# Hybrid decoder trunk on one core: router under the output projection, expert outputs added tile by tile, final norm on VectorE

## The reference

```
h = h + gla_mixer(rms_norm(h, a_norm), ...)             # layer 1: stick_breaking_mixer(...)
t = rms_norm(h, m_norm[layer])
g_logits = t @ w_group + b_group                        # 4 groups, top 1
e_logits = t @ w_expert + b_expert                      # 16 experts, top 2 inside the group
for e in range(16):
    hdn = silu(t @ w_gate[e]) * (t @ w_up[e])           # 1024 -> 512
    y = y + combine[:, e:e+1] * (hdn @ w_down[e])       # 512 -> 1024
h = h + y
...
return rms_norm(h, final_norm)
```

## Time and profile before

| | |
|---|---|
| Median of 3 runs | 1294.38 us (1287.04, 1294.38, 1294.63) |
| Profiled execution, its own time | 1287.17 us |
| Its span from first to last instruction | 1285.6 us |
| PE busy | 1149.8 us (89%) |
| DVE busy | 830.1 us (65%) |
| ACT busy | 692.4 us (54%) |
| POOL busy | 150.3 us (12%) |
| Chain that ended last | PE 75%, DVE 9%, issue 7%, POOL 4% |

### The profile page before, as it was taken

One profiled execution on the slowest core, in us unless ns is written; L12 is line 12 of the kernel. 1 busy time (PEld: TensorE's weight loads), 2 busy tenths in 40 slices (PEclk: granted clock), 3 DMA queues, 4 the chain that ended last, 5 costly groups with the idle time before them and its releaser, 6 DMA issues.

```text
span 1285.6 us, 14592 instructions
## 1 busy us (share of the span) xinstructions
PE 1149.8 (89%) x5517; PEld 864.8 (67%) x5517; DVE 830.1 (65%) x843; ACT 692.4 (54%) x730; POOL 150.3 (12%) x166
## 2 busy tenths in 40 slices
PE   6999997955999999996899979989739999999992
PEld 4788875844777777774688867768627777777760
DVE  3554235276888888886523356652568888888856
ACT  3532332343877777775232226651427777777752
POOL 1200030012001010002000013430030110100012
PEclk9999988976999999998899999999859999999996
DMA  8542003118999999997112310003079999999934
GB/s 286 148 157 98 1 1 131 66 75 270 376 390 391 392 402 394 393 376 285 69 66 98 98 33 1 2 19 129 1 237 360 401 391 390 391 394 411 378 132 178
DMA packets 88948, 283.10 MB, mean 220 GB/s; under 512 B 11688, under 2 KB 11856, under 8 KB 88896
## 3 DMA queue, kind: packets, MB, share of 16 engines
q1 hardware_dynamic: 72016, 239.32, 49.5%
q0 software_dynamic: 10912, 38.67, 8.9%
q10 hardware_dynamic: 5968, 4.40, 1.0%
HBM read 259.96 MB, written 22.41 MB: 220 GB/s over the span
## 4 chain that ended last, share of the span: by engine, by line
PE 75%; DVE 9%; issue 7%; POOL 4%; ACT 2%; DMA 2%; POOLq 0%; DVEq 0%; ACTq 0%
PE ps L1293 22%; PE ps L1295 22%; PE ps L1294 22%; PE ps L1486 2%; PE ps L1311 1%; POOL xn_r L1879 1%; DMA pad<-output_table,pos 1%; DVE xn L868 1%; PE ps L1447 1%; DVE raw L1232 1%; PE ps L1514 1%; PE ps L1327 1%; DVE xT_lo L824 1%; DVE xn_r L1236 1%; POOL xn_r L1874 1%
## 5 line engine op out<-in xcount | busy, mean ns | idle before, releaser
L824 DVE TENSOR_TENSOR w_lo<-raw,w_hi 128x2048 fp32r<-128x2048 f32 x72 | 164.7, 2288 | 85.1 <-ACT w_hi L487 84.9
L487 ACT CAST w_hi<-raw 128x2048 fp32r<-128x2048 f32 x72 | 137.7, 1912 | 116.5 <-PE ps L1295 116.3
L1293 PE MATMUL ps<-w_hi,s_hi 128*96 128x512 f32 x384 | 154.9, 403 | 6.6 <-DVE s_lo L1001 6.6
L1293 PE MATMUL ps<-xT_hi,s_hi 128*96 128x512 f32 (+1 forms) x392 | 156.7, 400 | 3.5 <-DVE s_lo L1013 3.5
L824 DVE TENSOR_TENSOR xT_lo<-raw,xT_hi 128x2048 fp32r<-128x2048 f32 x64 | 146.1, 2288 | 19.4 <-ACT xT_hi L487 19.4
L1295 PE MATMUL ps<-xT_hi,s_lo 128*96 128x512 f32 (+1 forms) x392 | 155.4, 396 | 0.0
L1294 PE MATMUL ps<-xT_lo,s_hi 128*96 128x512 f32 (+1 forms) x392 | 154.4, 394 | 0.0
L1295 PE MATMUL ps<-w_hi,s_lo 128*96 128x512 f32 x384 | 152.9, 398 | 0.0
L1294 PE MATMUL ps<-w_lo,s_hi 128*96 128x512 f32 x384 | 152.2, 396 | 0.0
L487 ACT CAST xT_hi<-raw 128x2048 fp32r<-128x2048 f32 x64 | 122.0, 1912 | 38.6 <-PE ps L1295 38.5
L828 DVE SCALAR_TENSOR_TENSOR w_lo<-raw,gainT,w_hi 128x512 fp32r<-128x512 f32 x88 | 60.1, 746 | 111.9 <-ACT w_hi L491 111.9
(11 more groups left out here) (289 smaller groups left out, 2028.9 us busy)
## 6 DMA issues: line engine op xcount, KB each, us to landing
raw<-in_m_w_up SPq DMA_DIRECT2D x64, 1024.0 KB, 9.8
xn<-in_m_w_gate SPq DMA_DIRECT2D x60, 1024.0 KB, 10.4
raw<-in_m_w_down SPq DMA_DIRECT2D x60, 1024.0 KB, 10.8
raw<-in_a_w_in SPq DMA_DIRECT2D x12, 1024.0 KB, 6.2
output_table<-pad POOLq DMA_DIRECT2D x30, 384.0 KB, 6.4
raw<-in_w_kv SPq DMA_DIRECT2D x8, 1024.0 KB, 8.2
output_table<-zeros POOLq DMA_DIRECT2D x11, 384.0 KB, 8.7
raw<-in_a_w_out SPq DMA_DIRECT2D x4, 1024.0 KB, 5.2
```

What stands on the lines that cost most here:

```text
L487: se.copy(hi, raw_block).then_inc(A["hi_done"], 1)
L824: ve.tensor_tensor(lo, raw_block, hi, ALU.subtract).then_inc(V["lo_done"], 1)
L1293: te.matmul(o, a_hi, b_hi, start=start, stop=False)
```

## The change

Three parts, on all engines.

1. *Router under the projection.* `out_proj` does the output projection by token tile: both column halves of a tile, then the next. While tile j is computed, tile j-1, complete with its residual, is transposed (8 transposes into banks 0 and 1), copied in fp32 to `hT`, and multiplied by the router's weights in plain fp32 (8 products of 20 columns); root and bias are applied afterwards on VectorE (`logits_in`), the gain is folded into `r_w`. ScalarE and VectorE do square sum, root, product with gain and the store of each tile in `out_tiles`. The last two blocks of the projection get slots of their own. POOL takes no part.
2. *The router itself.* Choices come from comparing the members of each group of four with each other and counting. The list of tokens is made at once from rank and expert, with bf16 products; the places of overflow rows (`overflow_places`) and the weights of choices (`token_weights`) move between the splits of the first experts.
3. *Tails.* Each tile is added completely before the next. In layer 0 the last expert's rows alternate between two pairs of banks, and their products for tiles 2 and 3 stand inside `dense_first`; VectorE's split of block B+2 stands behind the adds. In layer 1 the rows of all four tiles use the eight banks at once, and VectorE does the products with the final gain, one of them with the root left to ScalarE.

The core of the diff:

```diff
-            return n if n < 2 else SPLIT_E + layer if n == 2 else (n + 1) % 2
+            return n if n < 2 else SPLIT_E + layer if n in (2, 14) else SPLIT_E + 1 - layer if n == 15 else (n + 1) % 2
...
-        ADDS = [(0, 0), (0, 1), (1, 0), (1, 1), (2, 0), (2, 1), (0, 2), (1, 2), (3, 0), (3, 1), (2, 2), (3, 2)]
...
         @block.tensor
-            dense(6, 12, False)
-            dense(7, 14, False)
+            def out_proj(layer):
...
+                for j in range(NT):
+                    half(j, 0)
+                    if j:
+                        h_transposed_to(j - 1, range(KT))
+                    if j < last:
+                        half(j, 1)
+                        if j:
+                            logits(j - 1, range(KT))
+                half(last, 1, two_tiles)
+                logits(last, range(BK))
+                h_transposed_to(last, range(BK, KT))
+                logits(last, range(BK, KT))
...
         @block.vector
+            def out_tiles(layer):
...
+                for j in range(NT - 1):
+                    add(j, 0)
+                    add(j, 1)
+                    dve.wait_ge(A["half_squared"], squared + j + 1)
+                    ve.tensor_scalar(ms[:, j:j + 1], ss[:, j:j + 1], 1.0 / D, EPS, ALU.mult, ALU.add).then_inc(V["ms_ready"], 1)
+                    refine(j, j + 1)
+                    normed(layer, [j])
+                    if j:
+                        logits_in(j - 1)
...
             def experts(layer):
+                split(B + 1)
                 split(B + 2)
+                x_lo(E, I)
                 split(B + 3)
-                x_lo(E, I)
+                overflow_places(layer)
                 split(B + 4)
                 split(B + 5)
                 dve.wait_ge(M["blk_used"], B + 4)
                 mul(E, I, layer > 0)
                 x_lo(E, I + 1)
-                dve.wait_ge(M["last_tr"], layer + 1)
-                ve.tensor_copy(last_rows, ps[0:CAP, 7, :]).then_inc(V["last_out"], 1)
+                token_weights(layer)
                 split(B + 6)
                 split(B + 7)
...
+            combine(0, 0)
+            combine(0, 1)
+            tile_lo(3, 0)
+            combine(0, 2)
+            tile_lo(3, 1)
+            combine(0, 3)
             split(B + 2)
-            combine(0, 0, 8)
-            tile_lo(3, 0)
-            combine(0, 8, 12)
-            for i in range(1, NT):
+            for i in (2, 3):
                 tile_lo(3, i)
...
         @block.gpsimd
-                pool.wait_ge(G["gain_loaded"], 16 * (layer + 1))
-                for i in (2, 3):
-                    pool.wait_ge(A["xn_scaled"], 2 * layer + i - 1)
-                    ge.tensor_tensor(xn[:, i, :], xn[:, i, :], gain[:, :], ALU.mult).then_inc(G["xn_normed"], 1)
```

More of the change, by code:

```diff
@@ L348, in trunk, with out_banks, h_halves @@
         LAST = 4 + E_BLOCKS * (NE - 2)
+        def out_banks(j, half):
+            return ps[:, 4 + 2 * (j % 2) + half, :]
+        def h_halves(layer, j, half):
+            return 2 * NT * layer + 2 * j + half + 1
         def panel_banks(p):
@@ L1036, in step @@
                     mul(E, i)
+                    if first:
+                        dve.wait_ge(M["last_tr"], layer + 1)
+                        ve.tensor_copy(last_rows, ps[0:CAP, 7, :]).then_inc(V["last_list"], 1)
                     if more:
@@ L1172, in router, with combine @@
                 link(stt(base_k, tile_k, float(NE - 1), w12[:, :, :].rearrange("p k i -> p (k i)"), ALU.is_equal, ALU.mult))
-                link(tt(at_row, at_row, base_k.unsqueeze(2).broadcast_to([P, 2 * NT, CAP]), ALU.mult))
-                tt(at_row[:, 0:NT, :], at_row[:, 0:NT, :], at_row[:, NT:2 * NT, :], ALU.add).then_inc(V["last_ready"], 1)
-            def combine(layer, first, last):
-                for i, k in ADDS[first:last]:
+                link(tt(at_row, row_b[:, :, :], base_k.unsqueeze(2).broadcast_to([P, 2 * NT, CAP]), ALU.mult))
+                tt(at_row[:, 0:NT, :], at_row[:, 0:NT, :], at_row[:, NT:2 * NT, :], ALU.add).then_inc(V["last_list"], 1)
+            def combine(layer, i, terms=range(3)):
+                for k in terms:
                     if k == 0:
@@ L1295, in three, with transposed @@
                 return te.matmul(o, a_lo, b_hi, start=False, stop=stop)
[L1297 to L1302 removed]
+            def transposed(turn):
                 for k in range(KT):
@@ L1336, in rstd_row_sums, with dense_first @@
                 ins.then_inc(M["bc_done"], 1)
-            def dense_first(p, c, turn, event, first, between, between_half):
+            def dense_first(p, c, turn, event, first, between, between_half, behind=lambda i: None):
                 def half(j, n):
@@ L1515, in h_transposed, with lists @@
                 ins.then_inc(S["h_tr"], 1)
+            def lists(n_lists, bank, width):
+                pe.wait_ge(V["places_ready"], n_lists)
+                for n in range(2 * NT):
+                    ins = te.matmul(ps[0:CAP, bank, 0:2 * width], row_b[:, n, :], ids_b[:, n, :, 0:width],
+                                    start=n == 0, stop=n == 2 * NT - 1)
+                ins.then_inc(M["lists_done"], 1)
             def experts(layer):
@@ L1624, in router @@
                 ins.then_inc(M["ranks_done"], 1)
-                pe.wait_ge(V["places_ready"], 2 * layer + 2)
-                for n in range(2 * NT):
-                    ins = te.matmul(ps[0:CAP, 4, 0:TILES], at_row[:, n, :], at_tile_t[:, n, :], start=n == 0,
-                                    stop=n == 2 * NT - 1)
-                ins.then_inc(M["lists_done"], 1)
-            pe.wait_ge(V["r_lo_done"], 1)
-            transposed(2, 1, logits)
+                lists(2 * layer + 1, 4, NE)
+            out_proj(0)
             router(0)
@@ L1741, in _ @@
                     early_scores(q + 2)
-            pe.wait_ge(V["oT_lo_done"], 8)
-            dense(14, B + 12, False)
-            dense(15, B + 14, False)
-            pe.wait_ge(V["r_lo_done"], 2)
-            transposed(5, 3, logits)
+            out_proj(1)
             router(1)
```

493 lines of the change are left out of this document (270 added, 223 removed).

## The result

The changed kernel takes 1251.85 us (median of 4 runs, 1247.92 to 1253.49) against 1290.99 us before (median of 4): ratio 0.969, interval 0.965 to 0.974. Timed again in five rounds it gave 1248.11 us, ratio 0.970 (0.968 to 0.972). The profiled execution took 1247.92 us, 39.3 us less than the 1287.2 of before; the prediction's sum was 40.4. The changed kernel was profiled twice; where its second profile (run `changed_again`) says something else than the first, both are given.

A forecast was written before the change was run, and what follows sets the result against it. The gap between projection and first expert matmul, 48.25 us with TensorE little used, was taken as what can shrink; 36.8 + 0.5 + 3.1 = 40.4 us from 1287.2 gave 1246.8, stated as 1249, range 1237 to 1264.

The forecast's parts named there:

- the price of the deferred places: Router: overflow places, 5.1 us, move from ahead of the gather to between splits of the first two experts.
- Projection not dense: Rival, chance 0.19: TensorE waits for copies in each projection tile or logits cost 2.8 us; 7 us a layer, 1261.
- Gain refilled: Rival, chance 0.03: experts paced by weight bytes, so an earlier first matmul waits for weights and nothing is won; 1285.
- slower: Rival, chance 0.02: VectorE's 9 us do not drain and each expert is longer; at 2 us on 28 steps, 1303.
- Cheaper: Rival, chance 0.14: no stall in experts (+4), no contention (+2), tail +4; 1237 us.
- sum of 40.4: Whole kernel: 36.8 us from two layers' routers, 0.5 from layer 0's tail, 3.1 from layer 1's end.
- The gather's 1.0 us: From token list to transposes: 1.0 us added for gate loads sharing the DMA engines, bounds 0 to 4.
- The give-back of 2.0 us a layer: First experts: TensorE waits 0.2, about 0.8 and 0.9 us behind the deferred VectorE work, 2.0 us a layer lost.
- The tail of layer 0: Last expert's rows to dense work's end: ends at 647.6 instead of 648.1, 0.5 us gained, ends -3 and +4.
- wait of 2.5 us ahead of tile 2's first half: Layer 0's tail: tile 3's addition waits for the last product, then the 2.74 us split, then xT_lo(2).
- cold half: Layer 0's tail: first half of dense work runs on a cold clock, +2.0 us; by a warm start the tail term would be 2.5.
- The end of layer 1: Tiles added one by one from 1256.25, last output at 1278.2 instead of 1281.3: 3.1 us gained.

The follow-up runs named there:

- e5: Changed kernel with overflow places put ahead of the token list again and token weights right behind it, ahead of all splits, in both layers; 1260.29 us.
- e6: Changed kernel with TensorE doing all transposes of h and logits behind the projection's last half instead of between its halves; 1274.36 us.
- e1: Changed kernel with VectorE doing nine small instructions of the overflow places ahead of the split that starts with the first gather; 1253.57 us.
- e2: Changed kernel with the two gate loads of expert 1 waiting for the first gather to land; 1259.12 us.
- e9: Changed kernel with the edits of e1 and e2 together; 1250.81 us.
- e8: Changed kernel with 24 unused 512-column matmuls ahead of the first expert's row transposes and 4 behind them, in both layers; 1246.86 us.
- e3: Changed kernel with the split of the panel's third block in layer 0's tail moved into VectorE's wait for tile 2's last product; 1244.53 us.
- e4: Changed kernel with both tails put back as before the change, the router left as changed; 1250.36 us.
- e7: Changed kernel with eight more fp32 matmuls per tile's logits, 128 stationary and two moving columns, result unused; 1278.61 us.
- e10: e3 with 28 filler matmuls ahead of tile 0's transposes in layer 0's tail and 16 behind them; 1243.19 us.

## Why the prediction was right, and where it was not

**Right.** The time (1249 foretold, 1251.85 measured), the reason and the size. The projection ends at 266.86 (last addition; foretold 266.4); logits cost 1.85 us a tile, 1.70 from start to start (1.78); routing starts at 270.6 (270.8); top-k takes 2.9 us, from 270.61 to 273.55 (2.8); the token list is out at 277.10 (277.4); the first expert starts at 286.10 (285.9). Counted from the projection's start, that is 20.1 us sooner in layer 0 and 19.4 in layer 1, for 20.4. e5 confirms the price of the deferred places (4.96 for 5.1) and e6 that the transposes and logits belong under the projection. *Projection not dense* is refuted by the 52.60 busy of 52.60 us. *Gain refilled* and *slower* are refuted by the experts' pace: from the fourth to the fifth expert's row transposes 17.94 us (332.83 to 350.77), as before, and ScalarE waits for no load from 300 to 573. *Cheaper* came in none of its parts in full. That the sum of 40.4 lies so near the 39.3 is partly luck: in this profile layer 0's router and experts came out 0.8 us and its tail 1.4 us worse than their terms, layer 1's router and experts 0.4 us and its end 0.5 us better. Two sums on the way do not add up as written. Eleven instructions at 0.19 us and 1192 elements at 960 a us are 3.3 us, not 2.8; the 2.9 measured lie between. And four times 1.0 us with 2 to 3 us a tile, for *projection not dense*, is 12 to 16 us a layer, not 7, so that rival would have been dearer than 1261.

**The gather's 1.0 us: too small, and the wrong one of two causes.** I named contention with the gate loads. It comes to light once POOL is quick (e1), but in the changed kernel the split beside POOL takes the whole time (3.21 us behind POOL's instruction, as without loads), the split alone does the same (e2), and the time only comes back when both go (e9). The measured term is 1.5 us in layer 0 and 1.75 in layer 1. The prediction lacked a look at what VectorE does while POOL issues: the trace of before had a gather of 2.36 us beside a split (301.57, above), and the earlier trace rows the reverse case, a VectorE instruction of 1.84 us beside POOL's product.

**The give-back of 2.0 us a layer: right sign, partly another cause.** From the first expert's first matmul to the last expert's transposes layer 0 took 282.97 us before, 285.40 after and 284.04 in the second profile; layer 1 284.07, 284.70 and 284.72. So 2.4, 1.1, 0.6 and 0.7 us are given back. Two parts lie in this. The steady one is behind the first expert: from the second expert's row transposes to the last expert 270.39 us before, 271.54 and 271.36 after, in layer 1 270.19 and 271.56, so 1.0 to 1.4 us are given back there, for 2.0. The other is not VectorE's queue but how long the first expert runs at half clock, and that is chance: its up projection took 12.6 us in layer 0 and 13.9 in layer 1 before, 13.9 and 13.1 after, 12.7 in layer 0 of the second profile (half clock for 5.9 us above, for 3.2 us there). With fillers (e8) this part comes back. TensorE's waits for VectorE grew by 0.5 us only (0.7 to 1.2); what makes up the rest of the steady part stays open.

**The tail of layer 0: 0.5 us foretold as gain, a loss of 0.8 to 2.8 measured.** The steps up to the dense start were exact: tile 0 was to be ready at 608.9 and dense work to begin at 613.9; with the 17.8 us added that the last expert's store is issued earlier (590.81 before, 573.00 after), the transposes' 591.00 and the dense start's 596.27 are 608.8 and 614.1. The wait of 2.5 us ahead of tile 2's first half was foretold and came (2.48). The step that failed is the one behind it: I charged a cold half (one at half clock) once, at the start, but behind the wait the clock has fallen too (0.79 from 616 to 624), and tile 2's first half takes 4.2 us, not 2.74. That is the 1.5 us missing in the first profile, and e3 gives it back together with the wait. The other profiles of this tail lose more, the second one with its whole first half at half clock (5.3 us).

**The end of layer 1: 3.1 foretold, 3.4 to 3.6 measured** (e4 and the two traces).

## What to carry to other kernels

A small, weight-load-bound product costs least between dense matmuls: there it needs no wait of its own and runs at their clock, whereas behind them it also pays for a falling one, twice its time in e6. It has to stay short there: with twice as much of it (e7) the dense matmuls behind it lost their clock. When a wait of TensorE is put into a sum, add the slower matmuls behind it, and look first for a split or a copy that stands in the queue behind the awaited step and would fit into an idle stretch ahead of it (e3: one moved line, 3.6 us). Ahead of a gather on the critical path, look at both of its resources, what VectorE does beside the issuing engine and who loads the DMA engines: here taking one away showed nothing as long as the other held.

## What the runs showed of the hardware that I had not expected

- A GpSimd indirect gather of 96 rows took 0.90 to 1.05 us to issue beside an idle VectorE or its small instructions, and 2.74 to 2.96 us when it began just behind the start of a 2.28 us subtraction with two SBUF inputs; beside two of these in a row one took 4.70 us (315.55 in the changed kernel). It ended some 0.8 us behind theirs.
- TensorE can be busy in every microsecond and still lose its clock: 3.5 us of fp32 matmuls with 2 and 20 moving columns were followed by matmuls at half speed (0.84 over 11 us), 1.7 us of them were not.
- Whether the clock falls behind the same wait of 1.7 us ahead of the last down projection differs from run to run of nearly the same program: 1.00 in the changed kernel, 0.55 in e10. From the last expert's transposes to the product of its rows it takes either 9.2 us or 10.8; of the 26 times in the 13 profiles without fillers there, 9.2 came 9 times and 10.8 17 times, in either layer, before the change and after it. And the first expert's stretch at half clock was 5.9 us in one profile of the changed kernel and 3.2 in the next. That alone moves a total by 1 to 2 us, and it is why the stages were compared rather than the totals.
